# Gated feed-forwards: the product of gate and value moves from POOL to DVE for pairs 0 to 8

## What is computed

```python
D_FF_2 = 2816
def conv_glu_ffn(h, w_in, conv_w, conv_b, w_out):
    u = h @ w_in                                    # 256 x 5632
    up = jnp.pad(u, ((0, 0), (CONV_WIDTH - 1, 0), (0, 0)))
    u = sum(conv_w[k] * up[:, k:k + S] for k in range(CONV_WIDTH)) + conv_b
    gate, val = jnp.split(u, 2, axis=-1)
    return (jax.nn.gelu(gate, approximate=True) * val) @ w_out
```

## Time and profile before

| | |
|---|---|
| median of 3 runs | 891.98 us (890.57 to 893.31) |
| the profiled execution | 892.46 us, its span 890.7 us |
| PE busy | 860.7 us, 97% of the span |
| DVE busy | 621.9 us, 70% |
| ACT busy | 468.0 us, 53% |
| POOL busy | 145.5 us, 16% |
| DVE's first gate tile (L1973) of the first gated feed-forward | starts at 411.64 us |
| DVE's first gate tile (L1973) of the second | starts at 707.39 us |

### The profile page before, as it was taken

The page is one execution under the profiler, slowest core; times in us unless marked ns, Lnnn a source line. Parts: engine busy times, 40 slices in busy tenths (PEclk is TensorE's granted clock), DMA queues, the critical chain, the costliest instruction groups (busy, mean ns, idle before and its releaser), DMA issues.

```text
span 890.7 us, 15704 instructions
## 1 busy us (share of the span) xinstructions
PE 860.7 (97%) x6181; PEld 793.2 (89%) x6181; DVE 621.9 (70%) x816; ACT 468.0 (53%) x679; POOL 145.5 (16%) x132
## 2 busy tenths in 40 slices
PE   8999999998999999989999999999999989999997
PEld 8999888898999999869999999979777889999996
DVE  7787566769555555786776776877764677767776
ACT  5536766334444444465545555674665364555553
POOL 3272210007000000011121122000221111211100
PEclk9999999999999999999999999999999999999999
DMA  8953324623765555533555555434320545554541
GB/s 314 333 191 124 114 95 167 254 100 142 269 232 187 188 187 190 189 142 119 189 189 189 186 181 199 158 128 187 142 96 1 189 142 189 185 193 174 182 163 48
DMA packets 23065, 152.56 MB, mean 171 GB/s; under 512 B 2443, under 2 KB 3683, under 8 KB 5475
## 3 DMA queue, kind: packets, MB, share of 16 engines
q1 hardware_dynamic: 21648, 145.44, 46.3%
q10 hardware_dynamic: 1363, 6.37, 1.9%
HBM read 150.71 MB, written 1.09 MB: 170 GB/s over the span
## 4 chain that ended last, share of the span: by engine, by line
PE 66%; DVE 7%; ACT 3%; issue 1%; POOL 0%; DVEq 0%; POOLq 0%; ACTq 0%
PE up L980 12%; PE up L979 12%; PE up L978 12%; PE down L984 7%; PE down L985 7%; PE down L986 7%; DVE w_lo L1571 2%; PE up L1392 1%; PE down L1054 1%; PE down L1052 1%; ACT w_hi L629 1%; PE down L1489 1%; PE down L1200 1%; PE down L1058 1%; ACT proj L796 1%
## 5 line engine op out<-in xcount | busy, mean ns | idle before, releaser
L1571 DVE TENSOR_TENSOR w_lo<-w,w_hi 128x2048 fp32r<-128x2048 f32 x132 | 314.0, 2383 | 64.0 <-ACT w_hi L629 63.8
L978 PE MATMUL up<-x_lo,w_hi 128*128 128x256 f32 x1224 | 349.4, 285 | 0.9 <-DVE w_lo L1571 0.9
L979 PE MATMUL up<-x_hi,w_hi 128*128 128x256 f32 x1224 | 346.3, 283 | 0.0
L980 PE MATMUL up<-x_hi,w_lo 128*128 128x256 f32 x1224 | 346.2, 283 | 0.0
L629 ACT ACTIVATE w_hi<-w 128x2048 fp32r<-128x2048 f32 x132 | 251.6, 1908 | 74.0 <-PE down L986 31.7
L978 PEld LDWEIGHTS up<-x_lo,w_hi 128*128 128x128 f32 x1224 | 234.6, 192 | 3.2 <-DVE w_lo L1571 1.1
L979 PEld LDWEIGHTS up<-x_hi,w_hi 128*128 128x128 f32 x1224 | 234.7, 192 | 1.3
L980 PEld LDWEIGHTS up<-x_hi,w_lo 128*128 128x128 f32 x1224 | 234.6, 192 | 0.0
L984 PE MATMUL down<-w_hi,mid 128*128 128x512 f32 x256 | 101.0, 395 | 4.8 <-DVE mid L2003 2.4
L985 PE MATMUL down<-w_hi,mid 128*128 128x512 f32 x256 | 100.6, 393 | 0.0
L986 PE MATMUL down<-w_lo,mid 128*128 128x512 f32 x256 | 100.1, 391 | 0.0
(11 more groups left out here) (258 smaller groups left out, 1069.1 us busy)
## 6 DMA issues: line engine op xcount, KB each, us to landing
w<-w_stream SPq DMA_DIRECT2D x134, 1024.0 KB, 4.8
gates<-vec_store ACTq DMA_DIRECT2D x5, 1024.0 KB, 4.8
region<-rpb SPq DMA_DIRECT2D x2, 768.0 KB, 12.2
gates<-x_in SPq DMA_DIRECT2D x2, 512.0 KB, 4.4
result<-res SPq DMA_DIRECT2D x4, 256.0 KB, 2.0
con<-consts SPq DMA_DIRECT2D x1, 801.0 KB, 7.8
proj<-bands ACTq DMA_DIRECT2D x1, 544.0 KB, 4.2
gates<-vec_store ACTq DMA_DIRECT2D x1, 512.0 KB, 4.2
```

The costliest lines, as they stand in the source:

```text
L978: m(out_ap, w_hi[slot][:, w_cols:w_cols + P], xl, start=first, stop=False, skip_group_check=True)
L979: m(out_ap, w_hi[slot][:, w_cols:w_cols + P], xh, start=False, stop=False, skip_group_check=True)
L980: return m(out_ap, w_lo[slot][:, w_cols:w_cols + P], xh, start=False, stop=last, skip_group_check=True)
L1571: v.tensor_tensor(lo_of(n), w32[s][:, :], hi_of(n).bitcast(F32), ALU.subtract).then_inc(w_lo_ready, 1)
```

## The change

POOL's 18 products go, and DVE's branch for the last two pairs becomes the rule for all: behind the weight residue, where there is one, DVE waits for the gelu, the convolution and the previous `mid_lo`, multiplies, and waits for its own product.

```diff
-            def glu_products(rounds, base):
-                def product(at, j, j0):
-                    pool.wait_ge(gelu_ready, at.pair(j + 1))
-
-                    pool.wait_ge(conv_ready, at.pair(j + 1))
-                    if j > j0:
-                        pool.wait_ge(mid_ready, PAIRS1 + at.pair(j))
-                    g.tensor_tensor(glu_m, glu_g, glu_c[1], ALU.mult).then_inc(mid_f32, 1)
-                product(STRAIGHT, rounds, rounds)
-                with pool.Fori(0, (PAIRS2 - 3) // 2) as i:
-                    at = Looped(i, 4, 2)
-                    product(at, rounds + 1, rounds)
-                    product(at, rounds + 2, rounds)
-
-            glu_products(0, U_GLU0)
...
-            glu_products(PAIRS2, U_GLU1)
...
                 if j < PAIRS2 - 2:
                     next_split(at, units[1])
-                else:
-                    dve.wait_ge(gelu_ready, first + j + 1)
-                    dve.wait_ge(conv_ready, first + j + 1)
-                    dve.wait_ge(mid_ready, PAIRS1 + first + j)
-                    v.tensor_tensor(glu_m, glu_g, glu_c[1], ALU.mult).then_inc(mid_f32, 1)
-                    dve.wait_ge(mid_f32, first + j + 1)
+                dve.wait_ge(gelu_ready, at.pair(first + j + 1))
+                dve.wait_ge(conv_ready, at.pair(first + j + 1))
+                dve.wait_ge(mid_ready, PAIRS1 + at.pair(first + j))
+                v.tensor_tensor(glu_m, glu_g, glu_c[1], ALU.mult).then_inc(mid_f32, 1)
+                dve.wait_ge(mid_f32, at.pair(first + j + 1))
                 dve.wait_ge(mid_hi_ready, PAIRS1 + at.pair(first + j + 1))
```

## The result

The changed kernel takes 894.75 us in the median (893.29 to 896.24, 8 runs), the kernel before in the same measurement 891.83 (890.57 to 893.31, 8 runs): ratio 1.0033, 95% interval 1.0021 to 1.0044. The ratio is estimated together with its interval and is not simply the quotient of the two medians, which is 1.0026 here; where the two differ, the interval decides. The forecast was 893.8, +1.82 us. Over both measurements the change costs +2.3 us: 20 executions of it have their median at 893.99, and 108 of the kernel before, measured beside the experiments, at 891.73.

The account below looks back on a forecast made before the run. PE was taken to bound the kernel, busy 860.7 of 890.7 us. Terms of +1.46 and +0.36, with 0 for the loop, gave +1.82 us on a median of 891.98: 893.8 us, range for 8 in 10 runs 891.6 to 896.3.

Parts of the forecast that it names:

- Pair 0 of the second feed-forward: Product queued behind the residue on DVE delays `mid` and PE's first sum, from 719.50 to 720.96: +1.46 us.
- The first feed-forward: At pair 0 `mid` stays hidden, but the next residue comes late for PE: 0.26 plus 0.10, +0.36 us.
- The pairs in the loop: Pairs 1 to 8 of both feed-forwards: `mid` 0.48 us earlier, unused by PE, DVE's added work covered: 0.
- The rivals of a gaining and of a losing loop: Looped pairs: 7.7 us gained if PE waited for `mid`, chance 0.04; +6 if DVE delays a residue, chance 0.06.
- POOL, loads, everything outside, 0: Later weight loads hidden by 2.7 us, POOL earlier at its variance waits, nothing outside the feed-forwards moves: 0.
- My sum keeps it as it is: Second feed-forward, pair 0's sum: the low clock behind PE's wait, costing 1.7 us, keeps its length after the change.
- The first rival: Pair 0's sum, second feed-forward: clock low for twice as many matmuls, another 1.7 us, +3.5 in all, 895.5; chance 0.18.
- The second: Same sum: low clock falls into PE's wait or not at all; 0.8 instead of 1.46, +1.2 in all, 893.2; chance 0.12.
- No change, or slower?: Whole kernel: chance 0.71 of a time within 0.3% (2.7 us), 0.24 of slower, 0.05 of faster.

Follow-up runs that it names:

- e2: Kernel before with only pair 0's product of both feed-forwards moved to DVE, POOL keeping pairs 1 to 8: 894.06 us, ratio 1.0028.
- e3: Kernel before with the products of pairs 1 to 8 moved to DVE, POOL keeping pair 0 in both feed-forwards: 892.18 us, ratio 1.0002.
- e11: Kernel before with all products on DVE in the second feed-forward only, POOL keeping the first: 893.86 us against 891.52, ratio 1.0025.
- e10: Kernel before with all products on DVE in the first feed-forward only, POOL keeping the second: 891.34 us, ratio 0.9998.
- e12: e3 with four more unused products on DVE in each of pairs 1 to 8: 891.46 us against the kernel before's 891.52, ratio 0.9999.
- e8: e4 with the second feed-forward's first sum reordered on PE, rounded parts first, `mid_lo` last: 893.81 us against the kernel before's 891.77, ratio 1.0030.
- e7: e8 plus, in the second feed-forward, residues of units 5 to 7 one step earlier and pair 1's product ahead: 888.35 us against 891.77 before, ratio 0.9968.
- e9: The changed kernel measured a second time, unchanged, against the kernel before: 893.85 us against 891.52, ratio 1.0018.
- e4: The changed kernel with pair 0's product placed ahead of the weight residue on DVE: 892.04 us against the kernel before's 892.06, ratio 0.9999.
- e1: The kernel before, unchanged, against itself, to see its spread and mean granted clock: 891.53 us against 892.06, ratio 0.9995.

## Why the prediction was right

- **Pair 0 of the second feed-forward, +1.46 us.** Measured +1.46; `mid` starts 1.45 us behind the product (718.78, 720.23), PE at 720.98 against my 720.96, wait 3.85 against 3.86. e2, e3 and e11 put the loss there.
- **The first feed-forward, +0.36 us.** Measured +0.37 between 408 and 591 us, by the residue as worked out, with `mid` hidden. e10, in its profile, has the same 0.36 and nothing else between 432 and 705.
- **The pairs in the loop, 0.** 115.00 of 115.00 us, `mid` earlier by 0.55 (forecast 0.48) and of no use; e3 gives 1.0002 and e12 leaves room for five times the work. The rivals of a gaining and of a losing loop are both out.
- **POOL, loads, everything outside, 0.** Elsewhere PE's starts in the two traces keep their distance within 0.1 us, but for the low clock near 170 us, which is no effect of the change, and the 0.36 us at 687 to 691 us, which the next wait takes back.
- **The term that was left too small is the clock, as far as can be said.** "My sum keeps it as it is" took the one profiled execution, where the clock fell behind the 2.40 us wait, for all. It falls there in three of six profiled executions, and behind 3.85 us in four of four, and costs 0.7 us. By the estimate under e11 that adds 0.35 us to the median, which makes +2.2 of the forecast +1.82; against 2.3 measured this is plausible and not shown. The first rival, a longer slow stretch at +3.5, did not come: eight steps from matmul to matmul are at the low pace in both kernels, and in the changed one three at the full pace come before them. The second, that the clock gives back, had the size of a fall right, 1.46 - 0.8 = 0.7 us, and the wrong kernel: the fall is missing in some executions of the kernel before, and was there in all four with the longer wait. The Trainium skill's advice against long idle gaps between matmul bursts (TensorE: Matmul & The Clock Gate, "Why this matters for your kernels") agrees with the four falls behind 3.85 us; behind 2.40 us the fall came in half of the cases.
- **What was luck.** That the second measurement lands on 893.85, next to the forecast 893.8, is luck: the kernel before beside it was at 891.52, 0.46 below the 891.98 to which I added. The differences to compare with +1.82 are +2.9 and +2.3.
- **No change, or slower?** I gave 0.71 to within 0.3% and 0.24 to slower. The two measurements, +0.33% and +0.18%, lie on either side of 0.3%, and both intervals lie above 1: the change is slower, by about a quarter of a per cent, and which side of 0.3% it falls on is not settled. That changes below 0.3% can hardly be told was too careful; the intervals here reach 0.12% to either side.

## What to carry to other kernels

Moving an operation onto an engine that is free on average costs nothing where that engine waits for the bottleneck, and its full chain where the bottleneck waits for that engine. Here that was two places of eighteen, the first round of each feed-forward, where the steady state of the loop does not hold yet: look at the first round by itself. Before giving an operation up to the slot behind a long one, see whether the engine idles ahead of it; here the same move one slot earlier was free. And removing a wait pays only as far as the next thing that is late: e8 removed it alone and was slower, e7 moved the residues behind it too and was faster.

## What the hardware showed beyond that

- POOL's product took 1.3 us beside an idle DVE and 3.13 us when it met DVE's residue, ending 1.15 us after it. The Trainium skill (SBUF — State Buffer, "SBUF: two separate sides") says that GpSimd and a VectorE operation with two SBUF inputs exclude each other, the one that starts first holding the shared ports to its end; the trace agrees, since 1.15 us is close to the 1.3 that POOL takes alone. POOL's help in the loop was worth less than DVE's own 0.69 us.
- The same 2.4 us wait is followed by the low clock in some executions and not in others, and its price depends on what comes after: 0.7 us in front of a wait that was due anyway; 1.1 to 1.5 us near 170 us (6.0 or 6.4 us against 4.9, see e11); and near 593 us, where it falls behind waits of 1.2 us and less, 1.1 to 1.25 (from 591.37 to 600.04 in the kernel before it takes 8.7 us, in e9 and e11 9.8, in e4 9.9).
- The executions of one kernel differ by 1 to 2 us, and those with the lower mean clock are mostly the longer ones (e1). The falls near 170 and 593 us come and go in stretches that the edit of the run does not touch: near 170 us in ten of the fourteen profiled executions, near 593 in four, one of them e11, whose first feed-forward is that of the kernel before. What decides it in a given execution was not tried.
